# A two-layer streaming encoder: stores and some loads moved behind the cache attention

## The reference, cut to what matters

```python
for l in range(DEPTH):                                  # 2 layers
    # mixer: one input projection, then three mixers side by side
    qa, ka, va, ga, qb, kb, vb, qc, kc, vc = split_proj(rms_norm(h, norm_mix[l]) @ w_in[l])
    oa, ret_state = retention(rotary(qa), rotary(ka), va, state)      # group norm, times silu(ga)
    ob = sink_attention(qb, window(kb, 128 rows), window(vb), sinks)  # "swa": sliding window
    oc = bias_attention(qc, band(kc, 512 rows), band(vc), rel_bias)   # "ca": chunk band
    h = h + concat(oa, ob, oc) @ w_out[l]
    h = h + conv_ffn(rms_norm(h, norm_ffn[l]))          # the larger part of the matmuls
y = rms_norm(h, norm_final)
# the sample streams read their past from cache_swa_k/v (128 rows) and cache_ca_k/v (512 rows)
# outputs beside y: new keys and values, retention state, convolution tail, and the caches moved on
```

## Time and profile before

| | us |
|---|---|
| median of 3 runs | 1655.13 (1654.88 to 1656.14) |
| profiled execution | 1656.89 |
| its span, first to last instruction | 1655.3 |
| TensorE busy | 1582.9 (96%) |
| VectorE busy | 805.7 (49%) |
| ScalarE busy | 549.2 (33%) |
| GpSimd busy | 379.1 (23%) |

### The profile page before, as it was taken

The page is one execution under the profiler, slowest core; times in us unless marked ns, Lnnn a source line. Parts: engine busy times, 40 slices in busy tenths (PEclk is TensorE's granted clock), DMA queues, the critical chain, the costliest instruction groups (busy, mean ns, idle before and its releaser), DMA issues.

```text
span 1655.3 us, 27870 instructions
## 1 busy us (share of the span) xinstructions
PE 1582.9 (96%) x10866; PEld 1511.9 (91%) x10866; DVE 805.7 (49%) x1042; ACT 549.2 (33%) x818; POOL 379.1 (23%) x407
## 2 busy tenths in 40 slices
PE   6999969999999999999999997899999999999997
PEld 5899948999999999999978996589999999999997
DVE  5324667575554235554323256675655532455523
ACT  2332145334553123332222322362455521233311
POOL 6270010242221002222305401003422210122222
PEclk9999979999999999999999999899999999999998
DMA  5221271123332223222222215502223232332222
GB/s 185 71 77 52 112 271 52 39 69 115 114 114 100 71 84 126 101 68 75 78 96 70 83 39 209 213 1 69 89 101 127 93 96 78 113 118 73 72 72 89
DMA packets 44128, 160.45 MB, mean 97 GB/s; under 512 B 5760, under 2 KB 8224, under 8 KB 42976
## 3 DMA queue, kind: packets, MB, share of 16 engines
q1 hardware_dynamic: 40192, 129.11, 23.9%
q0 software_dynamic: 2464, 28.26, 4.0%
q10 hardware_dynamic: 1408, 2.17, 0.4%
HBM read 147.51 MB, written 30.88 MB: 108 GB/s over the span
## 4 chain that ended last, share of the span: by engine, by line
PE 87%; DVE 5%; ACT 3%; DMA 2%; issue 2%; POOL 0%; SPq 0%; DVEq 0%; ACTq 0%; POOLq 0%
PE PSUM L1383 61%; PE PSUM L1432 12%; PE PSUM L1457 7%; PE PSUM L1359 4%; DMA CAK<-ca_kt 2%; DMA RAW<-w_in 1%; DVE RS L878 1%; DVE XNL L886 0%; PE PSUM L1602 0%; PE PSUM L1448 0%; DVE PS L1072 0%; PE PSUM L1597 0%; DVE SM L1078 0%; DVE X L1344 0%; ACT WH L662 0%
## 5 line engine op out<-in xcount | busy, mean ns | idle before, releaser
L873 DVE TENSOR_TENSOR WL<-RAW,WH 128x1024 fp32r<-128x1024 f32 (+1 forms) x216 | 295.7, 1369 | 491.4 <-ACT WH L662 490.9
L662 ACT ACTIVATE WH<-RAW 128x1024 fp32r<-128x1024 f32 (+1 forms) x216 | 211.8, 980 | 606.1 <-PE PSUM L1383 408.5
L1383 PE MATMUL PSUM<-XFH,WH 128*128 128x320 f32 x1056 | 241.3, 310 | 1.8 <-DVE WL L873 1.2
L1383 PE MATMUL PSUM<-XFH,WL 128*128 128x320 f32 x1056 | 240.6, 309 | 0.0
L1383 PE MATMUL PSUM<-XFL,WH 128*128 128x320 f32 x1056 | 240.3, 309 | 0.0
L1383 PE MATMUL PSUM<-XNH,WH 128*128 128x320 f32 x864 | 198.3, 311 | 0.5 <-DVE XNL L1250 0.5
L1383 PE MATMUL PSUM<-XNL,WH 128*128 128x320 f32 x864 | 197.0, 309 | 0.0
L1383 PE MATMUL PSUM<-XNH,WL 128*128 128x320 f32 x864 | 196.9, 309 | 0.0
L1383 PEld LDWEIGHTS PSUM<-XFH,WH 128*128 128x128 f32 x1056 | 176.5, 188 | 3.1 <-issue 2.8
L1383 PEld LDWEIGHTS PSUM<-XFH,WL 128*128 128x128 f32 x1056 | 176.6, 188 | 0.0
L1383 PEld LDWEIGHTS PSUM<-XFL,WH 128*128 128x128 f32 x1056 | 176.5, 188 | 0.0
(11 more groups left out here) (208 smaller groups left out, 2362.3 us busy)
## 6 DMA issues: line engine op xcount, KB each, us to landing
RAW<-w_gu SPq DMA_DIRECT2D x88, 512.0 KB, 3.4
RAW<-w_in SPq DMA_DIRECT2D x40, 512.0 KB, 3.5
RAW<-w_down SPq DMA_DIRECT2D x32, 384.0 KB, 3.0
RAW<-w_down SPq DMA_DIRECT2D x32, 320.0 KB, 2.8
RAW<-w_out SPq DMA_DIRECT2D x16, 512.0 KB, 4.6
CAK<-ca_kt SPq DMA_DIRECT2D x16, 512.0 KB, 5.7
CAV<-ca_v SPq DMA_DIRECT2D x16, 512.0 KB, 4.1
ca_kt_copy<-ca_kt POOLq DMA_DIRECT2D x16, 512.0 KB, 4.8
```

What stands on the lines that cost most here:

```text
L662: nc.scalar.activation(WH[:, s, 0:width], RAW[:, s, 0:width], ACT.Copy).then_inc(hi_ready[s], 1)
L873: nc.vector.tensor_tensor(WL[:, s, 0:width], RAW[:, s, 0:width], WH[:, s, 0:width].bitcast(F32), ALU.subtract).then_inc(lo_ready[s], 1)
L1383: last = nc.tensor.matmul(PSUM[:, b + a, 0:HALF], w[:, s, P * k:P * (k + 1)], x[:, HALF * a:HALF * (a + 1)], start=start and k == 0 and w ...
```

## The change

Three things move; no buffer is added and no instruction goes or comes except waits. (1) POOL waits for the output of round 3 (unit 6) before it issues the five stores. (2) `SWK` and `SWV` are loaded behind the values of round 1, ahead of the keys of round 2. (3) Output units 0 and 1 are loaded behind round 3 with the other output units, and their `hi` and `lo` stand behind unit 9 (`OUT_WEIGHTS`) in the attention loops and no longer around the last retention step.

```diff
+        OUT_WEIGHTS = 9
@@ SP
                 sp.dma_start(STAB[:, :], rel_rows[l]).then_inc(rel_rows_loaded, 16)
-                load_unit(l, OUT_UNIT, w_out[l, 0])
                 ret_done.wait(sp, l, ("sample state", 2))
                 for b in range(2):
                     sp.dma_start(CAK[:, b, :, :], ca_kt[l, b]).then_inc(cak_loaded[b], 16)
                 sp.dma_start(CAV[:, 0, :, :], ca_v[l, 0]).then_inc(cav_loaded[0], 16)
-                sp.dma_start(SWK[:, :, :], swa_kt[l]).then_inc(swa_loaded, 16)
-                load_unit(l, OUT_UNIT + 1, w_out[l, 1])
                 in_copied.wait(sp, l, FEATURES - 1)
                 sp.dma_start(CAV[:, 1, :, :], ca_v[l, 1]).then_inc(cav_loaded[1], 16)
-                sp.dma_start(SWV[:, :, :], swa_v[l]).then_inc(swa_loaded, 16)
                 for r in range(1, 4):
                     for b2 in range(2):
                         if b2 == 0:
...
                         sp.dma_start(CAV[:, b2, :, :], ca_v[l, 2 * r + b2]).then_inc(cav_loaded[b2], 16)
-                for n in range(2, KT):
+                    if r == 1:
+                        sp.dma_start(SWK[:, :, :], swa_kt[l]).then_inc(swa_loaded, 16)
+                        sp.dma_start(SWV[:, :, :], swa_v[l]).then_inc(swa_loaded, 16)
+                for n in range(KT):
                     load_unit(l, OUT_UNIT + n, w_out[l, n])
@@ POOL
+                att_done.wait(pool, l, ("cas out", 3))
                 in_copied.wait(pool, l, FEATURES - 1)
                 token_ready.wait(pool, l, (VALUES, SAMPLE))
                 pool.dma_start(feat_out[l], F[:, :, :]).then_inc(attention_stored, 16)
@@ ACT
-                hi(l, OUT_UNIT)
                 take_retention(l, SAMPLE)
-                hi(l, OUT_UNIT + 1)
                 exps(l, ATT_UNITS[0])
...
                     for v in ATT_UNITS[n + 1:n + 2]:
                         exps(l, v)
+                    if n == OUT_WEIGHTS:
+                        for m in range(2):
+                            hi(l, OUT_UNIT + m)
@@ DVE
-                lo(l, OUT_UNIT)
                 retention_step(l, FEATURES - 1)
-                lo(l, OUT_UNIT + 1)
                 dve.wait_ge(rel_rows_loaded, 16 * (l + 1))
...
                     if n == 1:
                         finish_retention(l)
+                    if n == OUT_WEIGHTS:
+                        for m in range(2):
+                            lo(l, OUT_UNIT + m)
```

## The result

The changed kernel takes 1644.49 us (median of 20 executions, 1640.6 to 1655.48) against 1655.99 before (20 executions, 1654.18 to 1658.33): 11.5 us less, a ratio of 0.9939, 95% interval 0.9924 to 0.9954. The forecast was 13.35 us less, and 1641.8 as the time. (0.9 of the 2.7 us between the two times lies in the kernel before: the forecast started from the median of three runs, 1655.13.) Two things are to be explained: why the mechanism gave what it gave, and why the executions now spread over 15 us where they spread over 4.

A forecast was written before the change was run, and what follows sets the result against it. TensorE, busy 96% of the span, was taken as the bound, its big stall being round 1's `CAK` wait. Gain 19.35 less 3.6 and 2.4 gave 13.35 us: 1655.13 to 1641.8 us, range 1636 to 1650.

The forecast's parts named there:

- A: Round 1's `CAK` wait, both layers: with stores and other loads out of the queue ahead, 19.35 us gained.
- the second step of the working: Round 1, layer 0: VectorE starts some 1.45 us earlier, so ScalarE's copy of unit 0's transposes ends at 216.5.
- R4: Round 1's keys: stores are not the delay, the pair lands only at 219; 1652 us, chance 0.05.
- R3: Round 2's keys wait as round 1's did, so the stall moves; 1660 us, slower, chance 0.05.
- B: `SWK` and `SWV` ahead of round 2's keys delay unit 4's scores; 3.6 us lost, range 0 to 5.
- only four of the eight matmuls are left: Unit 4's scores, layer 0: first half done before the second lands, ready at 230.05 against 228.4, 1.65 us lost.
- R1: Round 2: the megabyte shows whole, 2.5 us plus 2 of low clock a layer; 1647 us, chance 0.14.
- R2: Losses from round 2's later keys and the moved `hi` and `lo` are covered; 1635.8 us, chance 0.10.
- C: Behind unit 9, `hi` and `lo` delay ScalarE's copy and unit 10's output; 1.2 us a layer, 2.4 lost.
- D: POOL's new wait and ScalarE's wait for the stores: covered by some 17 us or more, cost 0.
- The clock: TensorE's clock, an unknown of both signs: 2 us a layer back if high, as much lost by a further fall.

The follow-up runs named there:

- the long execution: Profiled execution of the changed kernel with no further edit, 1654.47 us; the kernel's median is 1644.49 us.
- the short execution: Profiled execution of the changed kernel run again without an edit, 1642.83 us; that run's median is 1645.73 us.

## Why the prediction was right

**A, the stores.** Right in mechanism and nearly in size: 9.3 + 9.2 = 18.5 us in the changed kernel against 19.35. In the long execution the second step of the working shows too: VectorE 1.35 us earlier, ScalarE's copy ending at 215.82 + 0.74 = 216.56, reckoned as 216.5. R4, that the pair would land late anyway, is refuted by the run with the stores alone, and R3, that the stall would move whole, by the 2.15 us of idle time.

**B, the megabyte ahead of round 2.** The place and the wait were right (2.15 us of idle time, 2.4 reckoned), the term was too small: 2.2 + 2.8 = 5.0 against 3.6. The step that failed took credit for the first half's matmuls being done before the second half lands, "only four of the eight matmuls are left". In the trace the scores start at 228.40 and go on over both halves; there was little to save. It is the other end of the range given, 5.0: the megabyte showed whole, which is the first half of R1; R1's further 2 us of low clock a layer did not come in the short execution. R2, that B is covered, falls.

**C, `hi` and `lo` behind unit 9.** 0.89 and 0.84, 1.7 in all, against 2.4; the way it was worked out (ScalarE's two copies less its idle time) holds, but the two take 1.90 us together and not 2.12. VectorE's `lo` are covered as said.

**D, the waits for the stores.** Nothing waits, as said: ahead of `hi` of output unit 2 ScalarE waits for a product, and SP goes on without a gap.

A - B - C as measured is 18.5 - 5.0 - 1.7 = 11.8 us, less than the 13.35. The short execution still gains 14.1 of profiled time (1656.89 - 1642.83), because the kernel before loses to the clock in two more places, which no term of the sum had: 1.7 us in layer 0 between units 3 and 9 (39.8 us against 38.1), and about 1 at layer 1's transposes of the mixed frames. That the short executions come so near the forecast is thus in part luck: the terms alone fall 1.6 short.

**The clock.** It was named as an unknown of 2 us a layer, and its fall was put down to the stop at the `CAK` wait. In the trace of the kernel before it falls sooner: the granted clock is 0.69 in the microsecond from 212 and 0.50 in the next, while TensorE still waits for ScalarE's probabilities:

```profile
213.31 1.12 PE L1618 MATMUL PSUM<-CONST,PC 128*128 128x128 f32 x4 [3.21 <-ACT PC L733]
```

That the clock could fall again in the tail wasn't reckoned with, and 2 us were too little: the deep fall cost 6.4 us in the long execution and 8 a layer with the gap widened. Such falls spread the executions, and with the short ones near 1642 it is they that put the median above the forecast, as far as the profiles go. Shown is that a longer gap ahead of unit 10's output brings the deep fall in both layers. That moving or filling the 0.8 us gap takes it away is likely and not shown (none of 20 long, against 2 of 11 beside them). Open is why that gap has the deep fall behind it in some executions only, and why the kernel with `SWK` and `SWV` early, which has it as well, had no long one in four.

## What to carry to other kernels

When a load lands late, look at what else is in the DMA queues at that moment, above all at stores that nobody waits for: one wait on the storing engine gave 16 us, and the reordering of loads without it lost 4. Move a load to where the queue has spare time, not just behind another load; a queue that ends within a fraction of a microsecond of its consumer has none. In a stretch where TensorE is fed by chains of small work, read the granted clock of several executions before a microsecond is moved between ScalarE and TensorE: 1.9 us of idle time added ahead of unit 10's output cost some 10 a layer.

## What the runs showed of the hardware

Once fallen, TensorE's clock stayed at its lower level for 17 us in the long execution and for 20 with the gap widened, while TensorE was busy some 90% of the time or more (4.53 of 5 us, and 5.00 of 5 from 285 to 290 us with the gap widened) with the matmuls and transposes of units 10 to 12; in the same instructions at the higher level it was busy 4.77 of 6 us and kept the clock. It rose again during the transposes of the mixed frames, 2 to 3 us ahead of the first output product: in the long execution the granted clock is 0.64 in the microsecond from 301 and 1.00 in the next, and TensorE had no idle time in either. The Trainium skill ("TensorE: Matmul & The Clock Gate", section "What's actually happening") says that the throttled state is the default and activity releases it. The rise agrees with that; the 5 us of unbroken work at the lower level show that a busy TensorE in the profile isn't enough to tell when it comes.

The stores take more than half of the bytes. With them in flight the pair of `CAK` of round 1 took 13.1 to 14.6 us to land, without them 4 to 5.7. From 210 to 222 us of the kernel before some 390 GB/s were moved in all. What each queue moved while the pair waited, from 213 to 220 us (queue 0 is POOL's with the stores, queue 1 SP's with the loads: packets, MB, share of the 16 engines):

```profile
q0 software_dynamic: 123, 2.42, 82.0%
q1 hardware_dynamic: 126, 0.49, 17.0%
```

The two queues sent as many packets as each other, but a packet of the stores was five times as large on average, and the loads got 17% of the bytes. The Trainium skill ("DMA: Bandwidth & Descriptors", section "Queues, rings and completion order") says that each DMA engine goes round between the queues it has work for, packet by packet. That agrees with these counts: a share by packets, and not equal shares of the bytes.
